# Hybrid decoder step on one core: unrolled layers, a last expert pair without a gather, and decode products in column groups of PE

## The chip, the core and the metric

The kernel runs on one core of a Trainium2 chip. The core has five engines with instruction streams of their own: PE (matmuls), ACT, DVE, POOL and SP, which here only issues transfers. They meet on semaphores. The metric is the device time of one execution in microseconds (us), the median of several runs; lower is better.

## What is computed

One inference step of a trunk with two layers, in float32, for 256 prompt tokens and 32 decode tokens (8 sequences of 4), 1024 wide. Cut to what matters:

```python
def _layer(x, c, pos, st, p, router_w, router_bias):
    mod = (jax.nn.silu(c) @ p["w_ada"] + p["b_ada"]).reshape(b, 6, D_MODEL)[:, :, None, :]
    sh1, sc1, g1, sh2, sc2, g2 = [mod[:, j] for j in range(6)]
    h = x * (1.0 + sc1) + sh1
    proj = h @ p["w_in"]
    z, xbc, dt_raw, rg_x, rg_gate, q, k, v, g = jnp.split(proj, ...)
    y_ssd, ssd_buf_new, ssd_h = _ssd_mixer(z, xbc, dt_raw, ssd_h0, ssd_buf, p)
    y_rg, rg_buf_new, rg_h = _rglru_mixer(rg_x, rg_gate, rg_h0, rg_buf, p)
    y_ret, ret_h = _retention_mixer(q, k, v, g, pos, ret_h0, p)
    mix = jnp.concatenate([y_ssd, y_rg, y_ret], -1) @ p["w_out"]
    x = _layernorm(ALPHA * x + (1.0 + g1) * mix, p["ln1_g"], p["ln1_b"])
    h2 = x * (1.0 + sc2) + sh2
    moe = _moe(h2, router_w, router_bias, p)      # 32 experts, top 2, blocks of tokens
    x = _layernorm(ALPHA * x + (1.0 + g2) * moe, p["ln2_g"], p["ln2_b"])
```

The ssd and retention mixers are recurrences with a state, `y_t = S_t^T q_t`. For each decode sequence the kernel reads its old state, multiplies its queries with it and writes the new state back. The condition c has 9 rows: one for the prompt and one for each decode sequence.

## The kernel before

**Tiles.** The tokens are tiles 0 and 1 (128 prompt tokens each) and tile 2, the 32 decode tokens (`TS`). All weights pass through a ring of slots in SBUF. In the mixers the ring has three slots of 2 MB, filled by SP at L575 in the order of the list STREAM: per layer 12 chunks of w_ada (128x8x512), 11 of w_in and 4 of w_out. SP waits for a slot's release by PE (`free_slot`) before it issues the next chunk into it. In the experts, two slots of gate, up and down weights follow at L581 and L586.

**Engines and order.** Each engine runs its own loop over the layers (`Fori(0, DEPTH)`: SP L557, POOL L625, PE L767, ACT L1438, DVE L1735). The order on each engine is the order of the code. Inside these loops the value that a wait compares with is computed from the layer's number in a register.

**Banks.** Most PE results go through PSUM banks 0 to 5 in rotation. `bank_plan()` lists them in order, each with its taker, ACT ("A") or DVE ("D"). `fills` is the wait for a filled bank, `takes` the wait for an emptied one, `emptied` the wait for the bank six entries back. Banks 6 and 7 are held for sums over the decode loop.

**A layer on PE, in order.**
1. Four `ada` products: `silu(c) @ w_ada`, 512 columns each. Eight 128x512 products (L785) run in four column groups of 32 rows of the bank. A last one (L788) adds the bias. c stands in 32 rows, 9 of them used; the sum over the four groups is taken later, by a product with a constant matrix ("fold" for the prompt's row, "gs" for the decode tokens).
2. `columns` (L814) turns the modulation into columns, `turn_x` (L824) turns x. For turn_x PE waits for `begun`, which DVE sends when the norm of the layer before is done.
3. w_in: L882 and L906. Between its products lie the mixers' parts. `ssd(2)` has a loop over the 8 decode sequences: L1036 multiplies with the old state (two 32x512 products, banks 6 and 7), L1044 makes the update, DVE applies it (L1953 to L1963), POOL writes the state and loads the one three sequences on.
4. `ret(0)` to `ret(2)`. ret(2) has such a loop too: L1161 (four 32x128 products, one per head, side by side in the columns of bank 6), L1169 for the update, and ada 6 to 11 between the steps.
5. `spread(c)` for c = 4 and 5: "mp" (L796) spreads the modulation over 128 prompt rows, "ms" (L799) over the 32 decode rows, each in a bank of its own. Then w_out: `mix(i, a)` for tile i, half a (L1220). For tile 2, L889 makes partial sums in four column groups, which ACT takes; L1216 and L1217 fold them. spread(6) to spread(9), taken by ACT at L1645 as shift and scale, the last mix, spread(10) and spread(11), taken at L1649 as the gate.
6. DVE's norm and modulation, products that keep PE busy (L1264), router logits (L1257), the routing on DVE.
7. Experts in pairs of blocks: gate and up (L1350), silu on ACT (L1673), product and turn on DVE (L2370, L2372), down (L1364). Between a pair's products, `gather` (L1325) picks the tokens of the next pair with a matrix `sel` from DVE (ending at L2308), ACT copies them to `xTb`. `spread_out` (L1379, L1383) adds the pair to the tokens. 14 pairs are fixed (in 7 quads), the rest is a loop (L1415) whose count comes from the routing: 2 pairs in the first layer here and 3 in the second. The last pair gathers too, though no pair follows.
8. Norm of the layer's end on DVE (to L2122), and back to step 1.

## Time and profile before

| | us |
|---|---|
| median of 3 runs | 2038.85 (2036.88 to 2039.37) |
| profiled execution, its own time | 2036.24 |
| its span, first to last instruction | 2034.7 |
| PE busy in the span | 1656.7 |
| DVE busy | 762.0 |
| ACT busy | 348.2 |
| mean DMA rate | 279 GB/s |

The mean granted clock of PE is 0.89 of full speed. The time of the profiled execution is 2.61 us below the median and 1.5 us above its span. Busy shares are a mean over stages of very different kinds: the two expert stretches (from about 540 and 1515 us on) move 428 GB/s, the mixers much less. So the stages are read one by one: the chain that ended last in order of time, then what each engine waited for in a window, then how long a transfer took from its issue to its landing.

### The profile page before, as it was taken

What the parts mean: (1) busy time and instruction counts of PE and PEld (TensorE: products, weight loads), DVE (VectorE), ACT (ScalarE), POOL (GpSimd) and SP (SyncE); (2) the same over time, 40 slices, a digit from 0 to 9 for tenths busy, and PEclk for the clock granted to TensorE, in tenths of its full rate; (3) what the DMA queues carried; (4) which work ended last, traced back from release to release, by engine and by line L of the source; (5) the groups of instructions that cost most, each with busy time, mean ns of one, the idle gap of its engine ahead of it and who ended that gap; (6) DMA issues with size and microseconds to landing.
All of it is one profiled execution on the core that took longest, in us unless ns stands there. A gap on an engine that the chain in (4) does not pass through costs nothing.

```text
span 2034.7 us, 30468 instructions
## 1 busy us (share of the span) xinstructions
PE 1656.7 (81%) x11526; PEld 891.8 (44%) x11526; DVE 762.0 (37%) x1701; ACT 348.2 (17%) x793; POOL 114.3 (6%) x162
## 2 busy tenths in 40 slices
PE   3999999899966766677799999989996776676783
PEld 1775533443533433344377553344353333343442
DVE  0264635537522211222526364553762211222225
ACT  1235211102111110111023521110211110011000
POOL 3001012010100000000020000201000000000000
PEclk9899899889988888888889999997998878888787
DMA  8332335472799999999853242648179999999991
GB/s 298 125 124 88 109 118 156 177 280 106 315 426 428 428 429 428 429 428 427 318 189 125 88 124 74 185 173 288 66 307 429 426 429 429 428 429 428 428 428 48
DMA packets 93468, 567.55 MB, mean 279 GB/s; under 512 B 7062, under 2 KB 7918, under 8 KB 68035
## 3 DMA queue, kind: packets, MB, share of 16 engines
q1 hardware_dynamic: 81666, 532.06, 64.2%
q0 software_dynamic: 11712, 34.32, 6.1%
q8 instruction: 54, 0.88, 0.2%
q14 instruction: 36, 0.29, 0.0%
HBM read 550.54 MB, written 15.81 MB: 278 GB/s over the span
## 4 chain that ended last, share of the span: by engine, by line
PE 56%; DMA 31%; DVE 5%; issue 3%; DVEq 1%; PEldq 1%; SPq 1%; ACT 1%; ACTq 0%; PEld 0%; POOLq 0%; POOL 0%
DMA ring<-in_exp_w_up 29%; PE ps L1350 10%; PE ps L882 8%; PE ps L906 8%; PE ps L1325 3%; PE ps L1220 3%; PE ps L1094 3%; PE ps L785 2%; PE ps L889 2%; PE ps L1364 2%; DMA ring<-in_w_ada 2%; PE ps L1379 1%; PE ps L1044 1%; PE ps L1169 1%; PE ps L1036 1%
## 5 line engine op out<-in xcount | busy, mean ns | idle before, releaser
L1350 PE MATMUL ps<-ring,xTb 128*32 128x256 f32 x4224 | 326.7, 477 | 232.0 <-DMA ring<-in_exp_w_up 212.3
L1350 PEld LDWEIGHTS ps<-ring,xTb 128*32 128x32 f32 x4224 | 162.4, 136 | 394.7 <-issue 349.3
L2370 DVE TENSOR_TENSOR hb<-sg,ps 128x128 f32<-128x128 f32 x66 | 25.0, 379 | 479.7 <-ACT sg L1673 479.7
L1325 PE MATMUL ps<-sel,h_tm 128*128 128x128 f32 (+3 forms) x1008 | 179.4, 305 | 0.0
L906 PE MATMUL ps<-ring,hT 128*128 128x512 f32 x384 | 172.3, 605 | 0.0
L882 PE MATMUL ps<-hT,ring 128*128 128x288 f32 x640 | 164.1, 415 | 5.1 <-ACT hT L1461 3.9
L1325 PEld LDWEIGHTS ps<-sel,h_tm 128*128 128x128 f32 (+1 forms) x1008 | 138.8, 190 | 57.3 <-issue 26.4
L882 PEld LDWEIGHTS ps<-hT,ring 128*128 128x128 f32 x640 | 122.9, 195 | 40.3 <-ACT hT L1461 4.2
L1364 PE MATMUL ps<-ring,hTb 128*32 128x256 f32 x2112 | 134.1, 397 | 0.0
L2378 DVE COPY ys<-ps 32x256 f32<-32x256 f32 x132 | 55.9, 424 | 180.0 <-PE ps L1364 178.7
L1673 ACT ACTIVATE sg<-ps 128x128 f32<-128x128 f32 x66 | 18.4, 278 | 588.2 <-PE ps L1350 588.2
L906 PEld LDWEIGHTS ps<-ring,hT 128*128 128x128 f32 x384 | 72.5, 193 | 101.3 <-issue 98.2
L1379 PE MATMUL ps<-ys,selw 128*128 128x512 f32 x152 | 76.6, 634 | 22.8 <-DVEq L2379 22.8
L1432 ACT ACTIVATE ys<-ps 32x256 f32<-32x256 f32 x132 | 49.4, 374 | 217.5 <-PE ps L1364 216.7
L785 PE MATMUL ps<-ring,cT 128*32 128x512 f32 x384 | 62.9, 787 | 25.5 <-DMA ring<-in_w_ada 18.1
L1364 PEld LDWEIGHTS ps<-ring,hTb 128*32 128x32 f32 x2112 | 63.6, 113 | 44.7 <-issue 5.1
L2396 DVE TENSOR_TENSOR acc<-acc,ps 128x512 f32<-128x512 f32 x76 | 52.3, 688 | 43.2 <-PE ps L1379 43.2
L1094 PE MATMUL ps<-ring,hT 128*128 128x512 f32 x128 | 56.3, 595 | 1.8 <-DVE h_tm L1974 1.8
L1807 DVE SCALAR_TENSOR_TENSOR cv<-raw,vecT,cv 128x312 f32<-128x312 f32 x96 | 52.2, 544 | 8.7 <-issue 1.8
L1379 PEld LDWEIGHTS ps<-ys,selw 128*128 128x128 f32 x152 | 25.0, 193 | 68.9 <-issue 43.0
L1960 DVE TENSOR_TENSOR h0s<-h0s,tbh 128x512 f32<-128x512 f32 x32 | 22.2, 692 | 76.1 <-PE ps L1044 72.8
L785 PEld LDWEIGHTS ps<-ring,cT 128*32 128x32 f32 x384 | 12.2, 131 | 58.4 <-issue 35.2
(412 smaller groups left out, 1808.3 us busy)
## 6 DMA issues: line engine op xcount, KB each, us to landing
ring<-in_exp_w_gate SPq DMA_DIRECT2D x66, 2048.0 KB, 18.7
ring<-in_exp_w_up SPq DMA_DIRECT2D x66, 2048.0 KB, 23.2
ring<-in_exp_w_down SPq DMA_DIRECT2D x66, 2048.0 KB, 24.7
ring<-in_w_ada SPq DMA_DIRECT2D x24, 2048.0 KB, 10.9
ring<-in_w_in SPq DMA_DIRECT2D x22, 2048.0 KB, 8.0
ring<-in_w_out SPq DMA_DIRECT2D x8, 2048.0 KB, 9.3
h0s<-in_state_ssd POOLq DMA_DIRECT2D x16, 512.0 KB, 6.7
out_ssd_s<-h0s POOLq DMA_DIRECT2D x16, 512.0 KB, 5.5
```

Source lines behind the costliest of these rows:

```text
L785: mm(o[32 * g:32 * g + 32, :], cT[:, k, :], w[:, k, :], start=(r == 0), stop=(r == 1 and g > 0), skip_group_check=True)
L882: last = mm(o[:, 0:T], w[:, k, m * P:(m + 1) * P], hT[:, k, :], start=(k == 0), stop=(k == KT - 1))
L906: last = mm(o[:, :], hT[:, k, T0[i]:T0[i] + P], w[:, k, :], start=(k == 0), stop=(k == KT - 1))
L1094: last = mm(o[:, :], hT[:, k, T0[i]:T0[i] + P], w[k // 4][:, k % 4, a * 512:(a + 1) * 512], start=(k == 0), stop=(k == KT - 1))
L1220: last = mm(o[:, :], y(k, i), w[k // 4][:, k % 4, a * 512:(a + 1) * 512], start=(k == 0), stop=(k == 7))
L1325: last = mm(o, h_tm[0:ROWS[i], i, k * P:(k + 1) * P], sel[0:ROWS[i], i, 0:n], start=(i == 0), stop=(i == NT - 1))
L1350: last = mm(ps[32 * j:32 * j + 32, b, 0:2 * P], xTb[:, k, m * BLK:(m + 1) * BLK], w[:, 0:2, k * D_EXPERT + j * P:k * D_EXPERT + (j + 1) * ...
L1364: last = mm(ps[32 * c:32 * c + 32, 2 + b, 0:2 * P], hTb[:, b, j * BLK:(j + 1) * BLK], w[:, 2, j * D_MODEL + c * 256:j * D_MODEL + (c + 1) ...
L1379: last = mm(o[:, :], selw[:, T0[i]:T0[i] + P], ys[:, a * 512:(a + 1) * 512], start=True, stop=True)
L1807: stt(c_, r_[:, j:j + CVW], tap(j), c_, ALU.mult, ALU.add)
L2378: cpy(ys[m * BLK:(m + 1) * BLK, c * 256:(c + 1) * 256], ps[32 * c:32 * c + 32, 2 + b, 0:2 * P])
L2396: tt(v, v, ps[:, 4 + j % 2, :], ALU.add)
```

## The change

1. **Layers unrolled.** All five loops over the layers are Python loops. Each wait has a constant, and no engine branches back.
2. **Start.** In the first layer SP issues the first three w_ada chunks right behind the constants, with no wait, and x, the router's weights and its bias behind them, on a semaphore of their own (`x_in`).
3. **Bias of ada.** The one 32x512 product becomes four of 32x128, one per column group.
4. **spread.** It takes a group of chunks, (4, 5), (6 to 9) or (10, 11): first all mp products, then the ms products side by side in the column groups of one bank. ACT's and DVE's takes follow in that order, each still an instruction of its own.
5. **ssd(2), ret(2).** The two products of a decode step (ssd) and the four (ret) go to column groups of bank 6. DVE takes the ret sum with four 32x128 instructions in place of one. `mix_few` does tile 2's folds for both halves side by side.
6. **Last pair.** It has no gather, no select and no copy. In the other pairs of the tail PE waits for `sel` only behind the first gate_up.

```diff
@@ bank_plan
-    out += [((w, c), "D") for c in (4, 5) for w in ("mp", "ms")]
+    out += [(("mp", 4), "D"), (("mp", 5), "D"), (("ms", 4), "D")]
...
-    out += [((w, c), "A") for c in range(6, 10) for w in ("mp", "ms")]
+    out += [(("mp", c), "A") for c in range(6, 10)] + [(("ms", 6), "A")]
...
@@ SP
-            with sp.Fori(0, DEPTH) as l:
+            for l in range(DEPTH):
...
+                    if l == 0 and n == NS:
+                        tokens_in()
                     if r:
                         sp.wait_ge(st_used[s].sem, st_used[s].at(l, r))
-                    else:
+                    elif l:
...
@@ PE, ada and spread
-                    mm(o[0:32, :], C("ident", 12, c, 1).to_broadcast([12, 32]), bias[:], start=False, stop=True,
-                       skip_group_check=True).then_inc(FL, 1)
...
+                    for g in range(4):
+                        last = mm(o[32 * g:32 * g + 32, g * P:(g + 1) * P], C("ident", 12, c, 1).to_broadcast([12, 32]),
+                                  bias[:, g * P:(g + 1) * P], start=False, stop=True, skip_group_check=True)
+                    last.then_inc(FL, 1)
...
+                    pe.wait_ge(*emptied(l, ("ms", cs[0])))
+                    o = bank(("ms", cs[0]))
+                    for j, c in enumerate(cs):
+                        last = mm(o[32 * j:32 * j + TS, :], C("gs"), ada_at(c), start=True, stop=True, skip_group_check=True)
...
@@ PE, decode loops of ssd(2) and ret(2)
-                                last = mm(ps[0:TS, 6 + g, :], CmB[:, g, b, :], h0s[b % 3][:, g * 512:(g + 1) * 512],
+                                last = mm(ps[32 * g:32 * g + TS, 6, :], CmB[:, g, b, :], h0s[b % 3][:, g * 512:(g + 1) * 512],
...
-                                last = mm(ps[0:TS, 6, h * P:(h + 1) * P], QmB[:, h, b, :], r0s[:, b % 3, h * P:(h + 1) * P],
-                                          start=(b == 0 and h == 0), stop=(b == DEC_BATCH - 1), skip_group_check=True)
+                                last = mm(ps[32 * h:32 * h + TS, 6, 0:P], QmB[:, h, b, :], r0s[:, b % 3, h * P:(h + 1) * P],
+                                          start=(b == 0), stop=(b == DEC_BATCH - 1), skip_group_check=True)
...
@@ PE, tail
+                def tail_pair(q, more):
                     d = pe.snap(pairs + STEADY + q)
                     pe.wait_ge(g_taken, steady + QUADS + 1 + q)
-                    pe.wait_ge(sel_ready, steady + QUADS + 2 + q)
                     for b in range(2):
                         gate_up(d, b, b)
-                        last = gather(4 * b, 4 * b + 4, 2 * BLK)
-                        if b:
-                            last.then_inc(gt_full, 1)
+                        if more:
+                            if b == 0:
+                                pe.wait_ge(sel_ready, steady + QUADS + 2 + q)
+                            last = gather(4 * b, 4 * b + 4, 2 * BLK)
...
                         down(d, b)
```

How the order on the engines moves. The first place is SP's start; before, it reads (L554 is the router's bias, L575 the ring of the mixers):

```order
L550 DMA con<-in_con 128x1990
L551 DMA x_tm<-in_x_prompt 128x2x1024
L552 DMA x_tm<-in_x_sample 32x1024
L553 DMA rw<-in_router_w 128x256
L554 DMA rbias<-in_router_bias 128x32
L557 UNCONDITIONAL_BRANCH
L557 ISA
L575 ISA
L575 DMA ring<-in_w_ada 128x8x512
```

and of the change:

```order
L550 DMA con<-in_con 128x1990
L581 DMA ring<-in_w_ada 128x8x512 x3
L554 DMA x_tm<-in_x_prompt 128x2x1024
L555 DMA x_tm<-in_x_sample 32x1024
L556 DMA rw<-in_router_w 128x256
L557 DMA rbias<-in_router_bias 128x32
L581 DMA ring<-in_w_ada 128x8x512
```

The first three chunks of w_ada now stand ahead of x and the router's parts, and the fourth behind them.

The second place is PE at the end of the mixer, from the folds of tile 2 (`h_tm`, `spare`) on; `qkvg` holds the adas' sums. Before, down to the second pair of mp and ms (two more pairs follow):

```order
L1216 MATMUL ps<-h_tm,con 32x512
L1217 MATMUL ps<-spare,con 32x512
L1211 REGISTER_ALU
L1213 REGISTER_ALU
L1216 MATMUL ps<-h_tm,con 32x512
L1217 MATMUL ps<-spare,con 32x512
L796 MATMUL ps<-qkvg,con 128x512
L799 MATMUL ps<-qkvg,con 32x512
L796 MATMUL ps<-qkvg,con 128x512
L797 REGISTER_ALU
L799 MATMUL ps<-qkvg,con 32x512
L794 REGISTER_ALU
```

and of the change, where the two folds, the four mp and the four ms products stand together and the last mix (L1225) follows:

```order
L1237 MATMUL ps<-h_tm,con 32x512 x2
L1240 MATMUL ps<-spare,con 32x512 x2
L804 MATMUL ps<-qkvg,con 128x512 x4
L808 MATMUL ps<-qkvg,con 32x512 x4
L1225 MATMUL ps<-ring,yrg 128x512 x4
```

The same products in another order: the ms products of a group now fill different rows of one bank, and no wait stands between them.

The third place is ACT behind the same spread. Before, with the root L1569 in the middle:

```order
L1645 ACTIVATE sh_118<-ps 128x64x8
L1642 REGISTER_ALU
L1645 ACTIVATE sh_118<-ps 32x64x8
L1642 REGISTER_ALU
L1645 ACTIVATE sh_118<-ps 128x64x8
L1642 REGISTER_ALU
L1645 ACTIVATE sh_118<-ps 32x64x8
L1566 ACTIVATE stat<-con 128x1
L1567 REGISTER_ALU
L1569 ACTIVATE stat<-stat,con 32x1
L1642 REGISTER_ALU
L1645 ACTIVATE sc_121<-ps 128x64x8
```

and of the change, where the root (L1595) follows the first two acts and the four of 32 rows come last:

```order
L1664 ACTIVATE sh_118<-ps 128x64x8 x2
L1592 ACTIVATE stat<-con 128x1
L1595 ACTIVATE stat<-stat,con 32x1
L1664 ACTIVATE sc_121<-ps 128x64x8 x2
L1664 ACTIVATE sh_118<-ps 32x64x8 x2
L1664 ACTIVATE sc_121<-ps 32x64x8 x2
```

Eight acts as before, the two behind `sh_118` for the decode tokens moved behind all of the prompt's.

## Rows read from the trace of the kernel before

**Rows 1.** the page, part 4: the chain that ended last, by engine.
```profile
PE 56%; DMA 31%; DVE 5%; issue 3%; DVEq 1%; PEldq 1%; SPq 1%; ACT 1%; ACTq 0%; PEld 0%; POOLq 0%; POOL 0%
```

**Rows 2.** the page, part 5: groups of instructions; the costliest.
```profile
L1350 PE MATMUL ps<-ring,xTb 128*32 128x256 f32 x4224 | 326.7, 477 | 232.0 <-DMA ring<-in_exp_w_up 212.3
```

**Rows 3.** windows at the start: busy by engine, then PEclk, DMA share, GB/s.
```profile
10.00:12.00 2.00, 0.00 (x0) 0.00 (x0) 0.00 (x0) 0.00 (x0) 0.12 (x1) 1.00 0.84 134
12.00:14.00 2.00, 0.29 (x3) 0.32 (x4) 0.00 (x0) 1.47 (x2) 0.00 (x0) 1.00 0.01 0
14.00:16.00 2.00, 0.70 (x7) 0.61 (x6) 0.23 (x1) 0.87 (x1) 0.24 (x1) 1.00 0.00 0
16.00:18.00 2.00, 0.00 (x0) 0.00 (x0) 0.00 (x0) 0.00 (x0) 1.94 (x4) 1.00 0.67 164
```

**Rows 4.** the chain in order of time (start us, us, what), first layer's ret(2).
```profile
386.83 1.85 PE ps L785 x16
388.69 0.97 PE ps L788 x2
...
407.70 1.84 PE ps L788 x2
...
417.84 1.06 PE ps L1161 x8
...
422.93 7.43 DMA r0s<-in_state_ret
...
430.40 1.91 PE ps L1161 x8
...
447.71 0.97 PE ps L799 x2
...
450.72 13.95 PE ps L1220 x32
```

**Rows 5.** the same chain, ssd(2), one decode step's two products.
```profile
274.95 1.83 PE ps L1036 x4
```

**Rows 6.** DMA issues from 438.6 to 439 us, median us to landing.
```profile
ring<-in_w_out SPq DMA_DIRECT2D x1, 2048.0 KB, 10.3
```

**Rows 7.** windows, columns as in rows 3, around the last weights of the mixer.
```profile
409.90:449.10 39.20, 36.25 (x199) 17.40 (x198) 12.10 (x20) 3.35 (x7) 7.50 (x10) 0.83 0.91 329
```

**Rows 8.** ACT in order of time, the acts behind the adas' spread.
```profile
480.95 4.04 ACT L1645 ACTIVATE sh<-ps 128x512 f32<-128x512 f32 x4 [10.77 <-PE ps L796]
```

**Rows 9.** the chain, last pair of the first layer and the layer's end.
```profile
978.19 3.79 PE ps L1325 x24
...
983.85 3.45 PE ps L1350 x64
...
998.36 6.02 PEldq L767
...
1004.54 0.04 PEldq L828
...
1026.26 1.80 PE ps L824 x8
```

**Rows 10.** DVE in order of time, last pair and norm (two windows).
```profile
988.18 0.31 DVE L2372 STREAM_TRANSPOSE hTb<-hb 128x128 f32<-128x128 f32 x1
...
1015.85 7.04 DVE L2122 TENSOR_TENSOR x_tm<-x_tm,lnp 128x1024 f32<-128x1024 f32 x6
```

**Rows 11.** DMA issues from 959.2 to 959.6 us.
```profile
ring<-in_exp_w_up SPq DMA_DIRECT2D x1, 2048.0 KB, 23.2
```

**Rows 12.** groups by line, gate_up behind an idle PE (943 us, 1981 us).
```profile
L1350 PE MATMUL ps<-ring,xTb 128*32 128x256 f32 x64 | 6.4, 586 | 4.2 <-DVEq L2308 4.2
...
L1350 PE MATMUL ps<-ring,xTb 128*32 128x256 f32 x64 | 3.7, 380 | 2.8 <-DVEq L2308 2.8
```

**Rows 13.** DMA issues from 1963.4 to 1963.8 us.
```profile
ring<-in_exp_w_up SPq DMA_DIRECT2D x1, 2048.0 KB, 21.8
```

**Rows 14.** the chain, last gate_up of the second layer.
```profile
1990.45 3.45 PE ps L1350 x64
```

More of the change, by code:

```diff
@@ L624, in _ @@
         def _(pool):
-            with pool.Fori(0, DEPTH) as l:
+            for l in range(DEPTH):
                 pool.wait_ge(small_room, l + 1)
@@ L766, in _ @@
             pe.reg_mov(before, 0)
-            with pe.Fori(0, DEPTH) as l:
+            for l in range(DEPTH):
                 pe.wait_ge(settled, l + 1)
@@ L845, in _ @@
                 pe.wait_ge(begun, l + 1)
+                if l == 0:
+                    pe.wait_ge(x_in, 16 * 4)
                 turn_x(0)
@@ L1198, in _ @@
                     ret(i)
-                for c in (4, 5):
-                    spread(c)
+                spread((4, 5))
                 pe.wait_ge(*takes(l, ("yrt", 1)))
@@ L1232, in _ @@
                              ).then_inc(FL, 1)
-                for i, a in MIX_ORDER[2:5]:
-                    mix(i, a)
-                for c in range(6, 10):
-                    spread(c)
+                mix(*MIX_ORDER[2])
+                mix_few()
+                spread(range(6, 10))
                 mix(*MIX_ORDER[5])
@@ L1240, in _ @@
                 n += 2
-                for c in (10, 11):
-                    spread(c)
+                spread((10, 11))
                 pe.drain().then_inc(mix_over.sem, 1)
@@ L1437, in _ @@
             act.reg_mov(before, 0)
-            with act.Fori(0, DEPTH) as l:
+            for l in range(DEPTH):
                 def take_rows(dst, key, i):
@@ L1695, in _, with tail_pair @@
                 tail = act.value_load(npi[0:1, 0:1], min_val=2, max_val=TAILMAX)
-                with act.Fori(0, tail) as q:
+                def tail_pair(q, more):
                     d = act.snap(pairs + STEADY + q)
@@ L1699, in _ @@
                         silu(d, b)
-                        if b:
+                        if b and more:
                             act.wait_ge(gt_full, tb + q + 1)
@@ L1703, in _ @@
                         take_down(d, b, b)
+                rest = act.snap(tail - 1)
+                with act.Fori(0, rest) as q:
+                    tail_pair(q, True)
+                tail_pair(rest, False)
                 act.reg_add(before, before, tail)
@@ L1733, in over @@
                 return ap.unsqueeze(axis).to_broadcast(sh)
-            with dve.Fori(0, DEPTH) as l:
+            for l in range(DEPTH):
                 dve.wait_ge(filled.sem, fills(l, ("vec",)))
@@ L1760, in mods @@
                         ts(dst[:, 0, sl], o[:, :], one, None, ALU.add).then_inc(TD, 1)
-                        dve.wait_ge(filled.sem, fills(l, ("ms", c)))
-                        o = bank(("ms", c))
-                        ts(dst[0:TS, 1, sl], o[0:TS, :], one, None, ALU.add).then_inc(TD, 1)
+                    dve.wait_ge(filled.sem, fills(l, ("ms", chunks[0])))
+                    o = bank(("ms", chunks[0]))
+                    for n_, c in enumerate(chunks):
+                        last = ts(gate[0:TS, 1, c % 2 * CH:(c % 2 + 1) * CH], o[32 * n_:32 * n_ + TS, :], one, None, ALU.add)
+                    last.then_inc(TD, 1)
                 for j in range(2):
@@ L2168, in _ @@
                         if i == 2:
-                            dve.wait_ge(*takes(l, ("ms", 9)))
+                            dve.wait_ge(*takes(l, ("ms", 6)))
                             modulate(0)
@@ L2428, in _, with tail_pair @@
                 D()
-                with dve.Fori(0, tail) as q:
+                def tail_pair(q, more):
                     d = dve.snap(pairs + STEADY + q)
-                    select(2 * BLK, 2 * BLK)
+                    if more:
+                        select(2 * BLK, 2 * BLK)
                     for b in range(2):
```

128 lines of the change are left out of this document (76 added, 52 removed).

## The prediction

> **What bounds the kernel now.** I read the page first. PE lies on 56% of the chain that ended last, DMA on 31% [rows 1]. The largest group, the experts' gate and up products at L1350, idles 212.3 us for the ring of weights [rows 2]. So there are two kinds of stretch. In the expert stream the weights set the pace, and a faster PE only waits longer. In the start, the mixers and the ends of the tails, PE or a chain through PE sets it, and time can be taken out. I therefore went by the chain in order of time, and at each edit asked what is late next: a transfer, ACT, or DVE.
>
> All sums stand against the profiled execution, 2036.24 us for a span of 2034.7. The median of the timed runs is 2.6 us higher, 2038.85; I subtract the gain from the median.
>
> **The start.** SP issues the first w_ada chunk only after silu, the turned c and PE's release. The DMA share is 0.84 in 10 to 12 us, 0.01 and 0.00 in the next two slices and 0.67 after [rows 3]. The hole is 0.3 + 2.0 + 2.0 + 0.7 = 5.0 us. Now three chunks are issued behind the constants, and x, the router's weights and its bias behind these; bytes are only reordered, and nothing needs x before PE's turn_x, some 50 us in. The fourth chunk waits for PE to release slot 0, which also moves forward, since PE then waits for a chunk and no longer for x. Gain 5.0, and 0.5 for the bias product of the fourth ada, the one behind the last wait: **5.5**. If the chunks' own order let DMA run dry before the fourth, a part of the 5.0 comes back: bounds 2 and 6.
>
> **The bias product.** One 32x512 product at L788 takes 0.97 us, at half clock 1.84. Eight 128x512 products in four column groups (L785) take 1.85 [rows 4], 0.23 each, a fourth of 0.97 alone: the groups run side by side. Four 32x128 pieces should then take about 0.5 with the issue of 8 instructions: 0.5 gained, 1.3 at half clock.
>
> **ssd(2).** A decode step's two products at L1036 take 1.83 [rows 5]. In two column groups 0.9. Of eight steps per layer four stand on the chain; before the others PE waits for DVE or loaded state, so they hide. 4 x 0.92 = 3.7 per layer, **7.4**. Bounds 5 and 9.
>
> **ret(2), its adas and the spread.** Two waits hide part of the gain here. ada 4 and 5 lie ahead of a wait for DVE: nothing. Up to 420 us PE would win 1.3 (bias at half clock), 1.3 and 0.7 (the four products of L1161, 1.91 at half clock and 1.06 at full) and 0.5: 3.8. What lies between there and 430.40 hides behind a state's load, 7.43 us on the chain. Behind it: L1161 three times, 1.3, 0.7 and 0.7, two biases 1.0, and 0.65 for the two ms products (0.97 each at 447.71, with their issue) side by side: 4.35, together 8.15 [rows 4]. But the products at L1220, at 450.72, need the second w_out chunk, issued at 438.75 and landed 10.3 later, at 449.1 [rows 6]. That leaves 1.6 of slack. DMA's share from the first of these issues to that landing is 0.91 of 39.2 us, 3.5 us short of full [rows 7]; that first issue, which follows ada 6, itself moves 1.3. The cap is 1.6 + 3.5 + 1.3 = 6.4 if all holes close and 2.9 if none does. I take 5.0, nearer the cap, since each issue follows a product that moves forward: **10** for two layers, bounds 5.8 and 16.3.
>
> **The end of the mixer.** By PE alone the four fold products of (2,0) and (2,1) would run in the time of two (an estimate of 0.8 each, from the 0.97 of a 512-column product), the group of four ms products would save three times 0.97, and the last pair 0.97: 5.5. But these banks are emptied by ACT: four acts take 4.04 us [rows 8], eight take 8.08 and a root lies between, in either order. After the change the root comes behind two acts, for DVE's (2,1) norm, and ACT is blocked in order until about 483.3 instead of running from 480.95; six acts more end at 489.8, 0.7 later than now, and DVE's modulation follows. Only the last six products, their two acts fewer waits, give back 0.9 to 2.3. I take **1** for both layers (0.5 each), bounds -2 and +5. The Trainium skill, "TensorEngine Tiling (Array Packing)", section PSUM Bottleneck, says that tiling speeds up TensorE but not the emptying of PSUM; by that rule alone this part would be 0, and ret(2) would stand, since the loop keeps its emptying.
>
> **The tail.** In the last pair, 3.79 us of gather go twice [rows 9]. Without them, down waits for silu, hidden and its turn: the last gate_up, from 983.85, ends 3.45 later at 987.30, and the turned tile is there at 988.49, and drained by 988.65 as I read it [rows 9, 10]: 1.35 us. So 2.44 net each, and the wait for DVE's select before the pair goes. But the last chunks' transfers become the floor. In layer 0 the up chunk of the last block was issued at 959.4 and landed after 23.2, at 982.6, against gate_up at 983.85 [rows 9, 11]. PE then idles over 4 us before it, and the gate_up of an earlier pair behind an idle of 4.2 took 6.4 us instead of 3.5 [rows 12]: 1.2 + 2.4 - 2.9 = **0.7**, 3.5 at full clock. In layer 1 the landing is 1963.58 + 21.8 = 1985.4 [rows 13], against 1990.45 [rows 14]: 5.05 + 2.4 = 7.5 at full clock, 4.6 at half. The idle is two pieces of 1.4; the gate_up behind 2.8 of idle ran at full clock [rows 12], L1161 behind the wait that ended at 430.40 at half [rows 4]. I take the middle: **6**.
>
> **The layer's end.** PE's branch back to L767 takes 6.02 us [rows 9]. Unrolled, it is gone, but DVE's norm ends at 1022.9 (L2122, 1015.85 + 7.04 [rows 10]) and turn_x, now at 1026.26, waits for it. The path from there is DVE's: 1026.26 - 1023.0 = **3.2**. DVE's own branch comes behind that signal. The Trainium skill, "Runtime: NRT & Kernel Launch", section Instruction fetch mechanics, says that a taken branch to a place outside the window held forces a fetch before anything runs, while straight code is fetched ahead; the row of 6.02 agrees. But PE's program doubles, and no row shows whether that fetching is hidden in the dense stretches; the first layer runs straight today, with no such pause.
>
> **Waits against constants.** A wait whose value is computed costs a register step, 0.04 us [rows 9] and the piece of issue after it, so 0.04 to 0.10. About 16 stand on the chain in a layer: 2 x 16 x 0.08 = **2.6**, bounds 1.3 and 3.
>
> **Sum.** 5.5 + 7.4 + 10 + 1 + 0.7 + 6 + 3.2 + 2.6 = 36.4 us. 2038.85 - 36.4 = 2002.4, say **2002**. The expert stream stays as it is: its start is 5 or more us nearer, but DMA sets its pace from its first chunks on, so what is won ahead of it is kept.
>
> **Rivals.**
> 1. *Given back in waits and clock.* Where PE waits, it resumes at half clock. If the cap in ret(2) is 2.9, ssd(2) gives 2.5, and each mixer's end costs 1: 4 + 5 + 5.8 - 2 + 0.7 + 4.6 + 3 + 1.3 = 22. Time 2017 (2011 to 2027). For it: the bias of ada 6 at half clock, 1.84 [rows 4]. Against: most of the gains leave no idle behind.
> 2. *No cap.* The loads move with PE and the tails keep full clock: 6 + 8 + 16.3 + 5 + 3.5 + 7.5 + 3.2 + 3 = 52.5. Time 1986 (1983 to 1993). Against: the slack of 1.6.
> 3. *The column groups do not run side by side* (the pieces drain between tiles). Then ssd(2), ret(2), the bias and the ms products win nothing, 18.9 of the sum: 17.5 remain, time 2021. Against it L785 [rows 4].
> 4. *Slower.* After a longer wait for w_out PE resumes at half clock and keeps it through L1220 and the mixer's end. The stretch from 450.72 to 499.7 is about 49 us of PE work at full clock, 13.95 of it in the first row; each us of it at half clock costs one more. It beats the gain from 18 us per layer on; at 24 the time is 2050. Against: the half clock behind the wait at 430.40 was over at 447.71 [rows 4].
> 5. *The change does nothing*, within 0.2%: only if start and decode loops both hide.
>
> **Chances.** Forecast (1993 to 2011) 0.56; rival 1 0.18; rival 2 0.12; rival 3 0.05; rival 4 0.04; rival 5 0.03; slightly faster than before for other reasons 0.02. The range takes in rivals 1 and 2: 1986 to 2019, which leaves out about 2 in 10. A measurement tells 0.2%, 4 us, from no change: faster 0.93, same 0.03, slower 0.04.
>
> **What would show it.** DMA's hole at 12 to 16 us gone and the fourth chunk landing near 39; L1036's successor at 0.9 for four instructions; the bias at 0.5; w_out landing before L1220's successor begins, or PE waiting for it by name; ACT's eight acts still 8 us long; no pause of 6 us at the second layer, with turn_x waiting for DVE; the last gate_up behind a DMA. The forecast is wrong if PE's idle time turns up as half clock in the mixers, or if long straight code shows pauses of microseconds that name nothing.

## The result

The changed kernel takes 2024.33 us (median of 7 runs, 2019.42 to 2030.05), the kernel before 2036.88 (7 runs, 2033.06 to 2052.14). The ratio is 0.9922, with a 95% interval from 0.9894 to 0.9950: 12.5 us or 0.8% less, where 36 us were forecast, and above the upper end of the range, 2019. The profiled execution takes 2027.97 us, with a span of 2026.2 and a mean granted clock of 0.864, down from 0.890.

The page of the changed kernel, parts 1, 2, 4 and 5, answers to [rows 1, 2]:

```profile
PE 1626.1 (80%) x11574; PEld 881.1 (43%) x11574; DVE 761.2 (38%) x1701; ACT 347.1 (17%) x791; POOL 113.7 (6%) x162
...
PEclk8899988859888878888979989895989888888896
...
PE 46%; DMA 37%; DVE 9%; issue 2%; ACT 2%; DVEq 2%; SPq 2%; POOL 0%; ACTq 0%; POOLq 0%
...
L1367 PE MATMUL ps<-ring,xTb 128*32 128x256 f32 x4224 | 328.6, 479 | 238.9 <-DMA ring<-in_exp_w_up 233.5
```

PE now lies on 46% of the chain instead of 56%, and DMA on 37% instead of 31%. The idle time of the experts' product for its weights has grown from 212.3 to 233.5 us: the stream waits longer for its chunks.

The question is where the forecast gain went. So I cut both executions at the same seven places: the first product of the ssd(2) loop, the first of the y stage behind it (mix_a), the first of the ret(2) loop, the first with w_out (mix), the first router logits, the first expert product, and the end of the last spread_out. Lengths in us, first layer and second; in the row of the forecast the waits against constants (1.3 per layer) stand in the layers' first stretches, and the last three rows are experiments told of below:

| stretch | to ssd(2) | ssd(2) | to ret(2) | ret(2) | mix | routing | experts |
|---|---|---|---|---|---|---|---|
| before | 274.9, 249.0 | 64.2, 64.2 | 56.8, 56.6 | 54.7, 54.8 | 53.7, 53.7 | 33.6, 33.6 | 460.7, 494.6 |
| changed | 268.9, 243.1 | 68.9, 67.5 | 56.9, 54.8 | 54.6, 55.2 | 53.8, 53.9 | 35.1, 35.3 | 459.6, 489.4 |
| forecast difference | -6.8, -4.5 | -3.7 each | 0 | -5.0 each | -0.5 each | 0 | -0.7, -6 |
| ssd(2) undivided | 266.8, 243.1 | 63.8, 64.3 | 55.6, 55.8 | 53.9, 52.6 | 54.0, 54.6 | 35.2, 35.7 | 459.7, 489.5 |
| ret(2) filled | 267.2, 243.1 | 68.0, 68.0 | 57.2, 57.6 | 49.3, 48.4 | 53.8, 54.0 | 35.2, 35.4 | 459.5, 489.3 |
| all filled | 270.4, 243.1 | 65.1, 65.4 | 56.2, 56.9 | 52.8, 49.0 | 51.9, 53.6 | 30.5, 30.8 | 459.6, 488.0 |

The first stretches and the experts are about as forecast (the experts not for the forecast reason, see below). ssd(2) is longer instead of shorter: 8.0 us more in the two layers where 7.4 less were forecast. ret(2) gains nothing, 0.3 us more where 10 less were forecast. The routing is longer by 1.5 and 1.7 us. Against the forecast these three stretches lost 15.4 + 10.3 + 3.2 us, and that is the whole gap between the traced spans, which differ by 8.5 us and not by 36.4. The windows of these stretches tell why. First the kernel before, first layer: ssd(2), ret(2), mix, routing (columns: length, then busy time of PE, PEld, DVE, ACT and POOL, PEclk, DMA share, GB/s):

```profile
274.90:339.10 64.20, 60.74 (x181) 21.74 (x180) 26.45 (x43) 7.59 (x13) 15.01 (x13) 0.97 0.57 162
395.90:450.60 54.70, 51.21 (x252) 24.54 (x252) 17.79 (x35) 3.68 (x7) 9.76 (x13) 0.75 0.85 304
450.60:504.40 53.80, 52.34 (x157) 19.32 (x156) 38.45 (x54) 14.25 (x26) 1.11 (x2) 1.00 0.21 78
504.40:538.00 33.60, 29.54 (x147) 19.35 (x147) 23.27 (x99) 4.19 (x8) 8.83 (x16) 0.90 0.81 326
```

and the changed kernel:

```profile
268.90:337.80 68.90, 63.12 (x182) 25.07 (x181) 28.32 (x45) 7.23 (x11) 14.98 (x13) 0.83 0.56 158
394.70:449.30 54.60, 51.26 (x289) 22.36 (x289) 18.30 (x39) 3.97 (x8) 9.73 (x13) 0.53 0.85 304
449.30:503.10 53.80, 48.21 (x156) 19.90 (x155) 39.86 (x55) 13.78 (x25) 2.04 (x4) 0.94 0.31 122
503.10:538.20 35.10, 30.05 (x143) 19.73 (x142) 21.86 (x98) 4.06 (x8) 7.77 (x15) 0.85 0.63 243
```

PE's granted clock fell from 0.97 to 0.83 in ssd(2), from 0.75 to 0.53 in ret(2), from 1.00 to 0.94 in mix and from 0.90 to 0.85 in the routing. The clock is either full, 2.4 GHz, or half, 1.2 GHz. A stretch of length L with a mean of c had 2(1 - c)L us at half: 3.9 us in ssd(2) before and 23 after, 27 and 51 in ret(2). In ret(2) this is nearly all of the loop. PE is busy in 51.3 of its 54.6 us, so it looks like an engine at its limit, with the same length as before although its short products now run side by side.

### The profile page after: what moved, and what is told of

The parts are those of the page before. It is cut to its first block, busy times and chain, and to the rows that moved or that the text cites. A ratio compares the mean times of both kernels' runs of the same rounds, so it can differ in the third digit from the quotient of the medians.

```text
span 2026.2 us, 29151 instructions
## 1 busy us (share of the span) xinstructions
PE 1626.1 (80%) x11574; PEld 881.1 (43%) x11574; DVE 761.2 (38%) x1701; ACT 347.1 (17%) x791; POOL 113.7 (6%) x162
## 4 chain that ended last, share of the span: by engine, by line
PE 46%; DMA 37%; DVE 9%; issue 2%; ACT 2%; DVEq 2%; SPq 2%; POOL 0%; ACTq 0%; POOLq 0%
DMA ring<-in_exp_w_up 35%; PE ps L1367 10%; PE ps L894 8%; PE ps L918 8%; PE ps L1106 3%; PE ps L901 2%; PE ps L791 2%; PE ps L1056 1%; PE ps L1225 1%; PE ps L1181 1%; PE ps L1076 1%; PE ps L1342 1%; PE ps L1281 1%; DMA r0s<-in_state_ret 1%; DMA ring<-in_w_ada 1%
## 5 line engine op out<-in xcount | busy, mean ns | idle before, releaser
L1367 PE MATMUL ps<-ring,xTb 128*32 128x256 f32 x4224 | 328.6, 479 | 238.9 <-DMA ring<-in_exp_w_up 233.5
L918 PE MATMUL ps<-ring,hT 128*128 128x512 f32 x384 | 178.0, 621 | 0.0
L1342 PE MATMUL ps<-sel,h_tm 128*128 128x128 f32 (+1 forms) x912 | 163.2, 306 | 0.0
L1342 PEld LDWEIGHTS ps<-sel,h_tm 128*128 128x128 f32 x912 | 125.1, 189 | 53.8 <-issue 27.2
L1381 PE MATMUL ps<-ring,hTb 128*32 128x256 f32 x2112 | 129.9, 387 | 6.0 <-DVEq L2417 3.8
L791 PE MATMUL ps<-ring,cT 128*32 128x512 f32 x384 | 73.7, 907 | 26.5 <-DMA ring<-in_w_ada 24.5
L1381 PEld LDWEIGHTS ps<-ring,hTb 128*32 128x32 f32 x2112 | 62.7, 111 | 49.9 <-DVEq L2417 7.9
L1106 PE MATMUL ps<-ring,hT 128*128 128x512 f32 x128 | 56.5, 597 | 0.0
L1846 DVE SCALAR_TENSOR_TENSOR cv<-raw,vecT,cv 128x312 f32<-128x312 f32 x96 | 52.1, 543 | 7.2
L1396 PEld LDWEIGHTS ps<-ys,selw 128*128 128x128 f32 x152 | 24.2, 188 | 66.9 <-issue 41.1
L1056 PE MATMUL ps<-xw,BmB 32*128 32x512 f32 x64 | 37.9, 718 | 8.5 <-DVEq L1993 8.5
```

Of the source, the lines that this page charges most:

```text
L791: mm(o[32 * g:32 * g + 32, :], cT[:, k, :], w[:, k, :], start=(r == 0), stop=False, skip_group_check=True)
L918: last = mm(o[:, :], hT[:, k, T0[i]:T0[i] + P], w[:, k, :], start=(k == 0), stop=(k == KT - 1))
L1056: mm(o[:, :], BmB[:, b % 2, g * P:(g + 1) * P], xw[0:TS, g * 512:(g + 1) * 512], start=True, stop=True).then_inc(FL, 1)
L1106: last = mm(o[:, :], hT[:, k, T0[i]:T0[i] + P], w[k // 4][:, k % 4, a * 512:(a + 1) * 512], start=(k == 0), stop=(k == KT - 1))
L1342: last = mm(o, h_tm[0:ROWS[i], i, k * P:(k + 1) * P], sel[0:ROWS[i], i, 0:n], start=(i == 0), stop=(i == NT - 1))
L1367: last = mm(ps[32 * j:32 * j + 32, b, 0:2 * P], xTb[:, k, m * BLK:(m + 1) * BLK], w[:, 0:2, k * D_EXPERT + j * P:k * D_EXPERT + (j + 1) * ...
```

## What PE waits for now

The chain of the changed kernel in ret(2) answers to [rows 4]:

```profile
404.88 0.58 PE ps L794 x8
...
405.60 0.65 PE ps L1173 x8
406.25 2.00 PE ps L1181 x8
408.25 3.57 PE ps L791 x16
...
432.04 8.53 DMA r0s<-in_state_ret
...
449.34 5.78 PE ps L1225 x13
```

The pieces that the change touches are as short as forecast, even at half clock: the bias (L794) 0.58 instead of 1.84, the four products of L1173 0.65 instead of 1.91. But the ada product ahead of each bias (L791), which nothing touches, takes 3.6 us in all six steps. Before, one of the six took 3.6, two 3.3 and 3.1, and three 1.9 us, since the clock came back at about 416 us and again at 436. That alone is 6 us more. The state's load at 432.04 stands on the chain as before, with 8.53 us, but PE waits for it only 0.4 us: at half clock PE is slow enough to arrive with the state.

PE in order of time in ssd(2) of the changed kernel, the second decode step (in brackets the idle time ahead, and what ended it):

```profile
271.77 1.05 PE L1048 MATMUL ps<-h0s,CmB 128*32 128x512 f32 x4
274.71 3.77 PE L1056 MATMUL ps<-xw,BmB 32*128 32x512 f32 x4 [1.89 <-DVEq L1993]
```

and the same step with the products undivided (the experiment "ssd(2) in one group", below):

```profile
270.58 1.90 PE L1048 MATMUL ps<-h0s,CmB 128*32 128x512 f32 x4
273.52 2.21 PE L1056 MATMUL ps<-xw,BmB 32*128 32x512 f32 x4 [1.03 <-DVEq L1993]
```

The products of L1048 are 0.85 us shorter (1.05 against 1.90, [rows 5]). PE's wait for B from DVE (L1993) is 0.86 longer (1.89 against 1.03). All of the gain of this step is in the wait, and the four products of L1056 behind it, which the change leaves alone, take 3.8 us instead of 2.2.

Over the whole loop of the first layer, PE in order of time adds up. The eight pairs of products give 8 x 0.85 = 6.8 us. PE's waits grow by 2.2, from 3.4 to 5.6; two of them, 1.38 and 0.39, are new and for loaded states (`h0s`). Six groups that the change leaves alone are longer by 9.1 together, at half clock. -6.8 + 2.2 + 9.1 = +4.5, against 4.7 measured. So the waits alone would have left a gain of 4.6 us; the clock turned it into a loss.

At the end of the mixer and at the router's logits, ACT in order of time:

```profile
477.79 1.97 ACT L1664 ACTIVATE sh<-ps 128x512 f32<-128x512 f32 x2 [9.13 <-PE ps L804]
...
481.76 0.29 ACT L1595 ACTIVATE stat<-stat,con 32x1 f32<-32x1 f32 x1 [2.00 <-DVEq L1916]
...
483.72 2.19 ACT L1664 ACTIVATE sh<-ps 32x512 f32<-32x512 f32 x2
...
510.74 1.28 ACT L1687 ACT_TABLE_LOAD   x1 [1.68 <-PE ps L1274]
```

and PE's constant products ahead of the logits:

```profile
498.57 4.70 PE L1281 MATMUL ps<-con 128*128 128x512 f32 x6 [1.85 <-ACT hT L1458]
```

ACT takes the eight acts in the order read from the code, the root between. PE then waits 1.85 us for ACT, where before it waited for nothing; the constant products behind it take 4.70 us instead of 2.77. The last ACT line is new. The sigmoid's table load of 1.28 us starts 1.68 us after ACT's last work, behind PE's logits (released by L1274). Before, it ran ahead of them:

```profile
510.34 1.28 ACT L1656 ACT_TABLE_LOAD   x1
511.96 0.23 ACT L1656 ACTIVATE rt<-ps 128x64 f32<-128x64 f32 x1 [0.34 <-PE ps L1257]
```

The start and the layer's end, on the chain of the changed kernel, answer to [rows 3] and [rows 9]:

```profile
9.33 10.75 SPq L554
...
23.55 16.53 DMA ring<-in_w_ada
```

(the start) and

```profile
1020.64 1.12 DVE x_tm L2164
...
1021.90 1.97 PE ps L834 x8
```

SP is held for 10.75 us by x's transfer (L554) behind the three chunks, so the fourth is issued at 23.55; still it lands 4.25 us earlier than before, at 40.09 instead of 44.34. At the layer's end turn_x follows DVE's norm by 0.1 us, as forecast, and no pause of 6 us stands ahead.

## The experiments

Two theories: **clock** (the shorter products leave PE idle, and it then works at half clock on things that nobody touched), and **waits** (the gain only moves into waits for states and weights). Each kernel is read by its stretches in the table's sense. The experiments ran in three groups of four, each group on another chip; the kernel before, timed beside them, took 2039.5, 2044.45 and 2041.03 us. The ratios are against these. Single executions of one kernel differ by 10 us and more, so the stretches of the traces decide more than the medians; each kernel has one trace, with two layers in it.

### The changed kernel again

> The changed kernel once more, as the control for the three beside it. Two theories of where the forecast gain went. Clock: with column groups in the decode loops TensorE does not come back to full speed; its granted clock is 0.50 from 394 to 444 us in the first layer, and the products around it, which the change leaves alone, take twice as long. Waits: the gain of the products is real, but PE only arrives earlier at the loads of the old states, which POOL issues behind the stores. Both expect 2020 to 2028 us here, a clock of 0.50 in the ret loop of both layers, and the ratio near 0.992.

Measured: 2026.56 us, ratio 0.9935 (0.9911 to 0.9958). Stretches: ssd(2) 67.7 and 67.5, ret(2) 55.8 and 55.3, mix 54.0 and 53.9, routing 35.2 and 35.3. The lengths of ssd(2), mix and routing are those of the first trace, so they belong to the kernel. ret(2) is less fixed: its clock was 0.51 in the second layer, but 0.57 in the first, with 48 us at half instead of 54.

### ret(2) in one group

```diff
-last = mm(ps[32 * h:32 * h + TS, 6, 0:P], QmB[:, h, b, :], ...)
+last = mm(ps[0:TS, 6, h * P:(h + 1) * P], QmB[:, h, b, :], ...)
```

> The changed kernel with the four products of the ret(2) loop back in the columns of one group of rows, and DVE's one take of the sum. Clock: the granted clock is back at 1.0 in part of the loop, the ada products there take 1.9 us instead of 3.6, and w_out's first product starts 2 to 8 us earlier per layer; the time falls by 3 to 12 us below the changed kernel's. Waits: the products take 1.06 to 1.9 us instead of 0.65, all of it hides behind the state's load, and the time stays within 2 us of the changed kernel's, or is up to 4 us more.

Measured: 2036.54 us, ratio 0.9977 (0.9948 to 1.0007). ret(2) takes 53.9 and 54.0, with a clock of 0.69 in both: 33 us at half instead of 48 to 54. The clock does come back, and gains only 1 to 2 us, less than the 2 to 8 that the clock theory asked for. Neither theory expected the time, 10 us over the control. It stands in the routing, 41.1 and 41.2 us in place of 35.2: the gather behind it ran at half clock.

```profile
527.33 14.90 PE L1342 MATMUL ps<-sel,h_tm 128*128 128x128 f32 x48
```

The same 48 instructions took 9.0 in the changed kernel and 8.7 before, behind a wait of 2.3 to 2.4 us as here. In the 24 layers traced without fillers in the routing (two for each of 12 kernels), this gather took 14.9 us in six and 8.4 to 9.2 in the others, and the six include one layer of the kernel that is only unrolled, whose other layer took 8.5. So this edit is not needed for it. The twelve executions of the kernel here lie between 2021.33 and 2045.95 us; the traced one, 2044.63, is among the slow ones. Whether undividing ret(2) makes the slow gather more frequent, and what sets it for a wait of this length, no run shows.

### ssd(2) in one group

```diff
-last = mm(ps[32 * g:32 * g + TS, 6, :], CmB[:, g, b, :], ...)
+last = mm(ps[0:TS, 6 + g, :], CmB[:, g, b, :], ...)
```

> The changed kernel with the two products of the ssd(2) loop back in two banks and one group of rows. Clock: the windows 268 to 338 us go back from 0.70 to 0.78 to 0.88 to 1.0, and the first product of the y stage (mix_a) starts at the same distance from the loop's start as before the change, 64 us instead of 69; the time falls by 3 to 8 us. Waits: the loop's length is set by DVE, the state's store and the next load, and the time stays within 2 us of the changed kernel's or is up to 5 us more.

Measured: 2016.73 us, ratio 0.9895 (0.9868 to 0.9921), 10 us less than the control. ssd(2) is 63.8 and 64.3 us, the clock back at 0.97. With column groups and no filler it was 67.5 to 68.9 in all 14 layers traced. Undoing this edit is worth 3.2 to 4 us per layer, where doing it was forecast to be worth 3.7.

```profile
266.80:330.60 63.80, 60.77 (x181) 21.84 (x180) 26.46 (x43) 7.46 (x12) 15.00 (x13) 0.97 0.57 164
```

### The table load ahead

```diff
+f(stat[:, 62:63], C("eps"), ACT.Sigmoid)
 act.wait_ge(score_fill.sem, score_fill.at(l, 1))
```

> The changed kernel with one more ACT instruction, a sigmoid of a constant into a spare column, ahead of the wait for the router's logits. In the changed kernel the table load of 1.28 us starts 1.68 us late, once the logits are there; before the change it ran ahead of them. If a wait against a constant is carried by the table load and a wait against a register was not, this moves the load ahead again: 1.2 us less per layer, 2.4 us in all, and the sigmoid of the logits within 0.2 us of PE's end. If the load is late for another reason, no change.

Measured: 2026.77 us, ratio 0.9938 (0.9915 to 0.9961), no change in the median where 2.4 us were expected. In the trace the sigmoid now starts 0.18 us after the logits:

```profile
504.16 1.28 ACT L1684 ACT_TABLE_LOAD   x1
505.46 0.20 ACT L1684 ACTIVATE stat<-con 128x1 f32<-128x1 f32 x1
505.84 0.22 ACT L1688 ACTIVATE rt<-ps 128x64 f32<-128x64 f32 x1 [0.18 <-PE ps L1274]
```

The routing is 32.9 us in the first layer, 2.3 less, and 40.0 in the second, where the gather fell to half clock. The kernel that is only unrolled (below) also has the late load. So it comes with the unrolling. That a wait against a constant is carried by the table load itself, and one against a register was not, is the reading that fits; no run isolates it. The price is 1.2 us per layer, and it is most of the 1.5 to 1.7 by which the routing is longer.

### ssd(2) divided and filled

```diff
+mm(ps[:, 7, :], C("ident"), con[:, 0:512], start=True, stop=True)
 pe.wait_ge(Bm_ready.sem, Bm_ready.at(l, b + 1))
```

> The changed kernel with ssd(2)'s column groups kept and one product more per decode step: 128x512, of a constant, into the free bank 7, ahead of PE's wait for B (it runs 8 times a layer and is no part of the result). In the changed kernel the loop, from its first product to the y stage's first, takes 67.5 to 69 us, and 64 with the products undivided. If PE's idle time behind the shorter products is what brings half clock, the loop takes 63 to 65 us with the filler, although PE has 8 us of work more in it, and its windows show 0.9 to 1.0. If the column groups themselves are slow, or the loop waits for the states, it stays at 67 to 70 or gets longer.

Measured: 2025.26 us, ratio 0.9910 (0.9869 to 0.9950). The loop takes 68.5 us in the first layer and 65.2 in the second; the clock is 0.91 and 0.97. The second layer is as the clock theory has it, to 0.2 us: 8 us of work more, and 2.3 us less time. In both layers two waits of 0.8 for B were left behind the filler, and the waits for states are gone; only in the first layer did the products behind them fall to half for a time (12 us in all, by the clock of 0.91). So the second layer supports the theory, and the first is left open. The filler both shortens the idle time and adds dense work, and the run does not tell these two apart. In loops with undivided products, the kernels below among them, 3.8 to 9.2 us were at half clock in eleven of twelve layers, and 17 in the twelfth (70.4 us long, in the kernel that is only unrolled); in divided ones without the filler it was 20 to 23 us in all fourteen.

### No stores of the retention states

> The changed kernel without the stores of the new retention states of the decode sequences (8 of 256 KB per layer are left out, so the loads three steps on are issued at once). If the ret(2) loop is set by the chain update, store, load, the stretch from its first product to w_out's first, 54.6 to 55.8 us now, falls by 4 to 8 us. If it is set by PE at half clock, it stays above 53.

Measured: 2021.32 us, one run. ret(2) takes 52.4 us in the first layer and 55.3 in the second, where the clock was 0.51 throughout. Without the stores there is no chain from update over store to load, and in the second layer the loop is as long as with it, with PE at half clock: there the stores' chain is not what sets it. The first layer, 3.4 us below the control's 55.8, fits neither expectation. Its clock was 0.61, and kernels that keep the stores had divided loops of 49.7 and 51.5 us, so it is no evidence for the chain either.

### Unrolled only

> The kernel before with the five layer loops unrolled and nothing else. By the parts of the forecast: the stretch from the first layer's last spread_out to the second layer's first ssd(2) product 3 to 6 us shorter (248.9 before, 243.1 in the changed kernel); waits 1.3 us per layer less; the table load ahead of the router's sigmoid late by 1.2 us in each layer. Time 3 to 7 us below before.

Measured: 2033.51 us, ratio 0.9953 (0.9906 to 1.0001), so the time alone is not clear of no change. To the first ssd(2) 273.6 us, 1.3 less; from the first layer's end to the second ssd(2) 243.7, 5.2 less: together 6.5, against 5.8 forecast for the layer's end and the waits. Its experts take 490.7 us in the second layer, 3.9 less than before, which nobody expected. One routing was 41.0 us (gather at half clock), one ssd(2) 70.4 with two waits for state loads.

### ssd(2) undivided and the table load ahead

> The changed kernel with ssd(2)'s products undivided again and the sigmoid of a constant ahead of the wait for the logits, the two edits that shortened their stretches alone. If they add: 64 us for each ssd(2) loop, 1.2 us less from the logits to the first expert in each layer, and 10 to 14 us less than the changed kernel, 2012 to 2018 on a chip where before takes 2037 to 2040. If the clock gives back behind them, within 5 us of the changed kernel.

Measured: 2019.51 us, ratio 0.9886 (0.9852 to 0.9921). ssd(2) 65.5 and 65.5; ret(2) 49.7 and 52.0; routing 39.7 and 40.0, the gather at half clock in both layers. In this trace the two edits do not add: what is won ahead is lost in the routing. It is the slowest of the kernel's six executions (2024.65 us, against a lowest of 2015.6), so the slow gather in both layers need not be the rule. ret(2), which neither edit touches, was divided and without fillers here.

### Fillers at the mixer's end and in the routing

```diff
 for n_, i in enumerate(NORM_ORDER[:2]):
+    if n_:
+        keep_clock(2)
     pe.wait_ge(h2_ready.sem, h2_ready.at(l, n_ + 1))
...
+keep_clock(1)
 pe.wait_ge(*emptied(l, ("logit",)))
...
+keep_clock(2)
 pe.wait_ge(wdiag_ready.sem, wdiag_ready.at(l, 1))
```

> ssd(2) undivided, the sigmoid ahead, and five constant 128x512 products more per layer into bank 7, where PE waits for DVE or ACT: two ahead of the decode rows' turn at the end of the mixer, one ahead of the wait for the logits' bank, two ahead of the wait for the diagonals in the routing. Without them PE is idle there for 2.4, 1.9 and 2.4 us, the products behind run at half clock, and the gather behind the last wait took 8.3 to 9 us in some layers and 14.7 to 15.4 in others. Clock theory: the stretch from the logits to the first expert is 31 to 33 us in both layers (35.2 in the changed kernel, 39.7 and 40.0 without the fillers), the one from w_out to the logits 52 to 53 (54.0), and the time 8 to 14 us below the undivided one's. Rival: DVE and ACT set these stretches and the clock there is no matter: 33 to 34 for the first, 54 for the second.

Measured: 2001.55 us, ratio 0.9809 (0.9743 to 0.9875). The routing takes 30.5 and 30.8 us, mix 51.9 and 51.9, and both run at full clock throughout. Windows of mix and routing, first layer:

```profile
439.20:491.10 51.90, 48.79 (x162) 19.80 (x161) 38.07 (x53) 13.77 (x25) 1.09 (x2) 1.00 0.29 111
491.10:521.60 30.50, 28.47 (x151) 18.34 (x149) 23.57 (x100) 4.30 (x9) 8.72 (x16) 1.00 0.79 307
```

The five products add 4.9 us of PE work to a layer, nearly all of it in time that was idle, and take 11 us out of it against the kernel above, of which 6.4 are the slow gather of that trace. Against the changed kernel, whose gather took 9.0, mix and routing are 6.4 to 6.5 us shorter in each layer, 1.2 of them the table load. The median is 18 us below the kernel above, but on another chip; by the ratios to the kernel before, 0.9809 against 0.9886, it is 0.8%, some 16 us, and the intervals just touch. The gather took 8.5 us in all four layers traced with these fillers. The rival, that DVE and ACT set these stretches, falls.

### Fillers in ret(2) too

```diff
+mm(ps[:, 7, :], C("ident"), con[:, 0:512], start=True, stop=True)
 pe.wait_ge(Qm_ready.sem, Qm_ready.at(l, 1))
...
+if b < 2:
+    mm(ps[:, 7, :], C("ident"), con[:, 0:512], start=True, stop=True)
 pe.wait_ge(Km_ready.sem, Km_ready.at(l, b + 1))
```

> The same with three products more per layer in ret(2), one ahead of the first wait for the queries and one ahead of the first two waits for K. Clock theory: TensorE enters the loop's ada products at full speed, and the loop then waits for the weights' transfers, whose share is 1.0 for 45 of 52 us: 50 to 52 us for the loop, against 54.6 to 55.8 in the changed kernel. Rival, the loop is bound by loads alone and clock is no matter: 52 to 55, as in the kernel beside it. Time 2000 to 2010 where before takes 2037 to 2044.

Measured: 2000.35 us, ratio 0.9794 (0.9746 to 0.9843). It is 2% below before; that it is faster than the kernel above, 2001.55, is not shown. ret(2) takes 52.8 and 49.0 us; against the kernel above without these three products (52.1 and 53.2) the first layer is no shorter, and lies in the range of the rival.

### The changed kernel with fillers in ret(2) alone

> The changed kernel with only the three products in ret(2). Its loop takes 54.6 to 55.8 us in four of the six layers seen whose clock stayed at 0.50 throughout. Clock theory: 50 to 52.5 in both layers. If it stays at 54 to 56 with a clock of 0.50, the idle time before the loop is not what takes the clock away; the products in four column groups themselves are then the suspect, since with them undivided the clock came back to 1.0 after 20 us in every layer seen.

Measured: 2016.61 us, one run. ret(2) takes 49.3 and 48.4 us, in place of 54.6 to 55.8:

```profile
392.30:441.60 49.30, 37.51 (x292) 16.77 (x292) 16.71 (x30) 3.67 (x7) 9.75 (x13) 0.83 0.90 328
```

PE's busy time falls from 51.3 to 37.5 us, although three products more run. What is left is a wait for DMA: its share is 0.90 of the stretch, and the longest waits are for states,

```profile
408.90 0.43 PE L1174 MATMUL ps<-r0s,QmB 128*32 128x128 f32 x8 [4.53 <-DMA r0s<-in_state_ret]
...
429.19 0.65 PE L1174 MATMUL ps<-r0s,QmB 128*32 128x128 f32 x8 [5.69 <-DMA r0s<-in_state_ret]
```

So a loop shorter by the forecast 5 us does exist once the clock is back. But the cap that the forecast named, the second w_out chunk, does not set it: the chunk landed at 438.6, 3.0 us ahead of w_out's first product at 441.6, which waited for nothing. What holds the loop is the states' loads. And one execution is weak evidence for the size: in the 16 divided loops traced with their stores and without these fillers ret(2) took 49.7 to 55.8 us (mean 53.5), in the four with them 48.4 to 52.8 (mean 49.9), so the ranges overlap.

### The last pair gathers as before

> The changed kernel whose last expert pair gathers, selects and copies as before. The expert stretch takes 459.6 and 489.4 us in the changed kernel, 460.7 and 494.6 before, 460.0 and 490.7 in the kernel that is only unrolled. If the missing gather is worth what was forecast, 0.7 and 6 us, this gives 460.3 and 495; if most of the 5.2 us in the second layer came from elsewhere, 490 to 491.5.

Measured: 2020.39 us, one run. The experts take 461.7 and 489.5 us, against 459.6 and 489.4 in the changed kernel. The missing gather is worth 2.1 us in the first layer and 0.1 in the second. There the last gate_up starts 474.4 us after the first expert product in both kernels, behind the last up chunk. The changed one waits longer for it, and pays with the clock:

```profile
1982.09 6.14 PE L1367 MATMUL ps<-ring,xTb 128*32 128x256 f32 x64 [7.05 <-DMA ring<-in_exp_w_up]
```

The kernel whose last pair gathers, at the same place:

```profile
1974.53 3.66 PE L1367 MATMUL ps<-ring,xTb 128*32 128x256 f32 x64 [2.21 <-DMA ring<-in_exp_w_up]
1978.12 3.86 PE L1342 MATMUL ps<-sel,h_tm 128*128 128x64 f32 x24
```

The changed kernel has 3.86 us of gather less, and 2.5 us of gate_up and 1.3 of wait for the turned tile more.

Where the rest of the second layer's 5.2 us comes from, the kernel before shows. Its chunk landed no later, 474.7 us after the first expert product, but its PE came late: the last gate_up starts at 479.6. Ahead of it stood pieces at half clock, 3.64 us for a down of 1.93 and 5.76 for four spread_out products that otherwise take 3.94:

```profile
1967.14 3.64 PE L1364 MATMUL ps<-ring,hTb 128*32 128x256 f32 x32
1971.97 5.76 PE L1379 MATMUL ps<-ys,selw 128*128 128x512 f32 x8 [1.19 <-DVEq L2379]
...
1990.27 3.64 PE L1350 MATMUL ps<-ring,xTb 128*32 128x256 f32 x64
```

In the kernel that is only unrolled the same pieces of the last three pairs are 7.1 us shorter together, and PE waits for the chunk:

```profile
1994.09 3.66 PE L1350 MATMUL ps<-ring,xTb 128*32 128x256 f32 x64 [1.80 <-DMA ring<-in_exp_w_up]
```

All 13 other kernels reach the chunk, which lands 474.0 to 475.8 us after the first expert product; only the kernel before, in its one trace, does not.

## Why the prediction was wrong

By its steps:

- **The start**, 5.5 forecast. The fourth chunk lands 4.25 us earlier. The first ssd(2) product comes 6.0 us earlier, 4.5 to 11 in the executions of the kernels below that keep this start; 1.3 of it shows in the kernel that is only unrolled. Right within this scatter. The bound of 2 named the order of the chunks; SP's hold at L554 was not foreseen and cost little.
- **The bias**, 0.5 at full clock, 1.3 at half. It takes 0.42 and 0.58 to 0.65. Right.
- **ssd(2)**, 7.4. This step failed, and in its sign: the loops are 3.3 to 4.7 us longer each. The product's time was right (0.98 for two), but the working counted PE's pieces on the chain, took the waits behind them for fixed, and put the clock of what follows at nothing. In the first layer PE waits 2.2 us more, for B and for states, and the untouched pieces are 9.1 us longer, with 16 to 20 us more at half clock per layer. Undividing the products gives 3.2 to 4 back.
- **ret(2)**, 10. This step failed too: 0.3 us longer in place of 10 shorter. The term took the half-clock pieces of [rows 4] as given, 1.3 for each, and the full-clock ones between as safe. With the pieces short, the clock stayed at half for the loop, and each of the six ada products took 3.6 us. With three fillers it is 5.4 and 6.4 us shorter than before, the forecast size, in one execution. The cap was the wrong one: w_out's chunk was 3.0 to 3.7 us early, and PE waited for states. That the size of 5.0 was reached under another limit is luck in part.
- **The mixer's end**, 1. PE is 1.8 us earlier at the constant products (49.3 us from w_out's first product instead of 51.1), and these then take 1.9 more at half clock: 0. ACT's order and its eight acts were as worked out; the named risk, one of idle and clock, came true.
- **The tail**, 0.7 and 6. The experts are 1.1 and 5.2 us shorter, near the forecast. For the second layer the step named the floor, the up chunk's landing, and the half-clock gate_up (6.14 us at 1982.09); its own sum with that gate_up, 4.6, was a little closer than the 6 it took. But what it gave to the missing gather is not the gather's: of the 5.2 only 0.1 is. The trace of the kernel before stood 4.9 us behind the floor because of pieces at half clock, and 3.9 of the 5.2 shows in the kernel that is only unrolled. That the total fits is luck. In the first layer the gather is worth 2.1 where 0.7 was forecast.
- **The layer's end and the waits**, 3.2 and 2.6. turn_x follows the norm by 0.1 us. The unrolled kernel gives 6.5 for both. Right. No pause of straight code like the 6.02 us was seen.
- **The table load**, not in the forecast: 1.2 us per layer lost.

Rival 1, that waits and half clock give part back, is what happened. It had 0.18, with 22 us left and 2011 to 2027 as its range. Its arithmetic was as wrong as the forecast's, since it left ssd(2) a gain. Nothing in it said that a shorter product can make the work behind it slower. The rows to see it were there: the stretch from 396 us runs at half clock with PE busy, behind an idle time of 1.7 us, and so did the gate_up behind 4.2 [rows 12]. Of the kernel before, the first 5 us of ret(2):

```profile
395.90:400.90 5.00, 4.99 (x22) 3.97 (x23) 1.74 (x4) 0.00 (x0) 0.00 (x0) 0.50 1.05 394
```

I read them as places where pieces are longer. They were the price of idle time ahead of dense work, though not every idle time has it: the gate_up behind 2.8 ran at full clock [rows 12].

What stays open: why a wait of 2.4 us ahead of the routing's last products leaves the gather at 8.4 us in one layer and makes it 14.9 in another; why ssd(2) divided and filled was still 68.5 us in one layer; and whether it is the idle time alone that takes the clock away, or also how little PE works in the short products before it.

## What to carry to other kernels

Before dividing a short product, look at what PE waits for behind it: if it is another engine, the gain becomes idle time, and the dense work behind can run at half clock, which can cost more than was gained (here each ssd(2) loop became 3.3 to 4.7 us longer where 3.7 less were forecast). Try constant products in waits of about 2 us that stand ahead of dense work: five of them per layer, 5 us of work, made mix and routing 6.4 to 6.5 us shorter per layer than in the changed kernel (1.2 of it the table load), and the time of the kernel with ssd(2) undivided some 16 us less. After an unrolling, look at every table load of ACT: one that ran ahead of its wait may now stand behind it.

## What the runs showed of the hardware

- A busy PE says nothing of its clock: ret(2) was 94% busy at half clock and 76% busy at 0.83 of full in 5 us less.
- With the loops unrolled, where waits are against constants, ACT's table load of 1.28 us started behind the product that ACT waits for (510.74 against PE's end at 510.68); in the loop, with the wait against a register, it ran ahead (510.34, the product's end at 511.94).
- The same 48 instructions of the gather took 8.4 to 9.2 us in 18 layers and 14.9 in six, behind a wait of 2.2 to 2.7 us each time; with constant products in that wait, 8.5 in all four.
- SP was held 10.75 us in issuing a transfer of 1 MB while three chunks of 2 MB were under way ahead of it.
